# The w2 loads of an expert stage: issued by ScalarE behind the row copy in place of SyncE's queue

## The chip, the core and the metric

The kernel runs on one core of a Trainium2 chip. The metric is the device time of one execution in microseconds, lower is better. A core has TensorE (PE), VectorE (DVE), ScalarE (ACT), GpSimd (POOL) and SyncE (SP), each with an instruction stream of its own; they meet only at semaphores. SyncE, ScalarE and GpSimd can issue DMAs, and each has a queue of its own for them.

## What is computed

The kernel is one layer of a diffusion backbone for 640 tokens of width 1024: modulated normalisation, two attention branches, and then a mixture of 64 small SwiGLU experts with 8 experts per token. The change is in the last part alone:

```python
def swiglu(x, w1, w3, w2):
    return (jax.nn.silu(x @ w1) * (x @ w3)) @ w2

def run_block(args):
    xb, e = args                                   # 128 rows of one expert
    return swiglu(xb, w_e1[e], w_e3[e], w_e2[e])
...
return jax.ops.segment_sum(yd * wd[:, None], td, num_segments=t)
```

w1 and w3 are 1024 x 256, w2 is 256 x 1024, all in float32, so each is 1 MB, and no weight is used by more than one block unless an expert has over 128 rows.

## The kernel before

The stage around the change is the block that begins at L1707. It goes over 64 blocks of 128 rows, one for each expert, and then over overflow blocks for experts with more than 128 rows (in this run 70 blocks in all; the number `nb` is known only on the chip). For block n:

- GpSimd gathers its 128 token rows into `xg` (L1793), and three blocks later scatters the weighted output rows from `yb` into `sums` with an add (L1807). Rows that are empty in the block are left out.
- TensorE transposes the rows (`turn_x`, L1831), multiplies them with w1 and w3 (`up`, L1823 to L1825), transposes the product (`turn_g`, L1849) and multiplies it with w2 (`down`, L1843). In its program step n is: turn_x(n), down(n-2), turn_g(n-1), up(n).
- The multiplication with w1 and w3 is made of three products of rounded halves. ScalarE rounds x (`take_x`, L1879) and the weights (`hi_w13`, L1873), VectorE subtracts to get the rest (L1931, L1924).
- ScalarE also copies the output row block to `yb` (`take_y`, L1892), the transposed product (`take_g`, L1898), and computes silu (L1905). Its step n is: take_x(n), hi_w13(n+1), take_y(n-2), take_g(n-1), silu(n).

The weights go through a ring of four slots (`RING`), each with room for w1, w3 (one semaphore `s_w13[u]`) and w2 (`s_w2[u]`). SyncE issues all of these loads. Its step n waits until the up-projection of block n-4 is done (semaphore `u`) and issues two DMAs for w1 and w3 of block n (L1490); then it waits until the down-projection of block n-5 is done (semaphore `y`) and issues one DMA for w2 of block n-1 (L1494). For the overflow blocks (`late`, L1747) it reads the expert's number from memory (L1749), loads w1 and w3 of block n, and then waits for down(n-4) and loads w2 of block n.

The order in which the engines walk the blocks is in `run` (L1712): eight blocks are written out, blocks 8 to 59 are a hardware loop without conditions, and blocks from 60 on (`LAST` = 15, times four) are a loop in which each part of a step stands under a condition on `nb`.

Of the kernel before, what the change touches and what calls it, by code (L numbers as in the profile page):

```python
# [47 lines left out]
NE, TOPK, NG, TOPG = 64, 8, 8, 4  # L48
# [5 lines left out]
NBLK = NE + OVF  # L54
RING = 4
# [37 lines left out]
def build(nc, I, O, S, ctx):  # L93
    def sb(name, shape, dt=F32):
        return ctx.enter_context(nc.sbuf_tensor(name, shape, dt))

    def sem(name):
        return ctx.enter_context(nc.semaphore(name))
# [1154 lines left out]
    SH = RING - 1  # L1253
# [215 lines left out]
    ove = sb("ove", [1, P], I32)  # L1469
# [18 lines left out]
    def load_w13(sp, n, u):  # L1488
        for a in range(2):
            sp.dma_start(w13[u][:, a], w13_src[a][:, bass.ds(n, 1)].rearrange("p e k n -> p (e k) n"))\  # L1490
              .then_inc(s_w13[u], 16)

    def load_w2(sp, n, u):
        sp.dma_start(w2[u], w2_src[:, bass.ds(n, 1)].rearrange("p e f n -> p (e f) n")).then_inc(s_w2[u], 16)  # L1494
# [17 lines left out]
    se = {n: sem(f"s_e_{n}") for n in names}  # L1512
# [8 lines left out]
    def wslot(tab, n, w):  # L1521

        return tab[:, bass.ds(n, 1), w:w + 1].rearrange("p n w -> p (n w)")
# [183 lines left out]
    with nc.Block() as block:  # L1707


        LAST = NE // RING - 1  # L1710

        def run(eng, step):  # L1712

            for n in range(2 * RING):
                step(n, n // RING, n % RING, lambda k, n=n: None if n >= k else False)
            with eng.Fori(2, LAST) as i:
                for u in range(RING):
                    step(RING * i + u, i, u, lambda k: None)
            nb = eng.value_load(nblk[0:1, 0:1], min_val=NE, max_val=NBLK)
            with eng.Fori(LAST, NBLK // RING + 1) as i:  # L1720
                with eng.If(RING * i - 3 < nb):
                    for u in range(RING):
                        n = RING * i + u
                        step(n, i, u, lambda k, n=n: n - k < nb)
            return nb

        def due(eng, cond, what):
            if cond is None:
                what()
            elif cond is not False:  # L1730
                with eng.If(cond):
                    what()

        @block.sync
        def _(sp):

            def step(n, u):
                if not (isinstance(n, int) and n < SH):
                    if not (isinstance(n, int) and n < RING):
                        sp.wait_ge(se["u"], n - RING + 1)  # L1740
                    load_w13(sp, n, u)
                if not (isinstance(n, int) and n <= SH):
                    if not (isinstance(n, int) and n <= RING):
                        sp.wait_ge(se["y"], n - RING)
                    load_w2(sp, n - 1, (u - 1) % RING)

            def late(n, u):  # L1747

                e = sp.value_load(ove[0:1, bass.ds(n - NE, 1)], min_val=0, max_val=NE - 1)  # L1749
                sp.wait_ge(se["u"], n - RING + 1)  # L1750
                load_w13(sp, e, u)
                sp.wait_ge(se["y"], n - RING + 1)
                load_w2(sp, e, u)

            for n in range(RING + 1):
                step(n, n % RING)
            for u in range(1, RING):
                step(RING + u, u)
            with sp.Fori(2, NE // RING) as i:
                for u in range(RING):  # L1760
                    step(RING * i + u, u)
            sp.wait_ge(se["y"], NE - RING)
            load_w2(sp, NE - 1, RING - 1)
            nb = sp.value_load(nblk[0:1, 0:1], min_val=NE, max_val=NBLK)
            with sp.Fori(NE // RING, NBLK // RING) as i:
                with sp.If(RING * i < nb):
                    for u in range(RING):
                        n = RING * i + u
                        with sp.If(n < nb):
                            late(n, u)  # L1770

        @block.gpsimd
        def _(pool):
# [8 lines left out]
            def step(n, i, u, guard):  # L1782
# [29 lines left out]
                due(pool, guard(3), scatter)  # L1812

            nb = run(pool, step)

            pool.wait_ge(s_sc[0], (nb + 1) // 2 * 16)
# [3 lines left out]
        def _(pe):  # L1820
# [6 lines left out]
            def step(n, i, u, guard):  # L1827
# [35 lines left out]
                due(pe, guard(0), up)  # L1863

            run(pe, step)

        @block.scalar
        def _(act):
            def hi_w13(n, i, u):

                act.wait_ge(s_w13[u], 32 * (i + 1))
                for a in range(2):
                    act.activation(wHi13[u % 2][:, a], w13[u][:, a], ACT.Copy).then_inc(se["h13"], 1)  # L1873

            def step(n, i, u, guard):
                def take_x():
                    act.wait_ge(se["Tx"], n + 1)
                    for h in range(2):
                        act.activation(xHi[:, 4 * h:4 * h + 4, :].rearrange("p k t -> p (k t)"),  # L1879
                                       pX[:, 512 * h:512 * (h + 1)], ACT.Copy).then_inc(se["xh"], 1)  # L1880

                def next_w13():
                    if not (isinstance(n, int) and n == 0):
                        act.wait_ge(se["u"], n)
                    hi_w13(n + 1, i + (u + 1) // RING, (u + 1) % RING)

                def take_y():
                    m = n - 2
                    act.wait_ge(se["y"], m + 1)
                    if not (isinstance(n, int) and m < 2):  # L1890
                        act.wait_ge(s_sc[u % 2], 32 * i + 16 * ((u - 2) // 2))
                    act.activation(yb[u % 2], pY, ACT.Copy, scale=wslot(tabs, m, 2).bitcast(F32)).then_inc(se["ye"], 1)  # L1892

                def take_g():
                    act.wait_ge(se["Th"], n)
                    if not (isinstance(n, int) and n < 2):
                        act.wait_ge(se["y"], n - 1)
                    act.activation(gT.rearrange("p f t -> p (f t)"), pG[:, 0:256], ACT.Copy).then_inc(se["te"], 1)  # L1898

                def silu():  # L1900
                    act.wait_ge(se["u"], n + 1)
                    if not (isinstance(n, int) and n == 0):

                        act.wait_ge(se["g"], n)
                    act.activation(hs, pH[:, 0:FE], ACT.Silu).then_inc(se["sl"], 1)  # L1905

                due(act, guard(0), take_x)
                due(act, guard(-1), next_w13)
                due(act, guard(2), take_y)
                due(act, guard(1), take_g)  # L1910
                due(act, guard(0), silu)


            act.wait_ge(s_acc, 16 * NT)
            hi_w13(0, 0, 0)
            run(act, step)

        @block.vector
# [135 lines left out]
```

## Time and profile before

| | |
|---|---|
| median of the runs before | 1903.27 us (1901.7, 1903.27, 1909.15) |
| the profiled execution, its own time | 1898.28 us |
| its span, first to last instruction | 1896.5 us |
| PE busy | 1688.7 us, 89% of the span |
| ACT busy | 698.6 us, 37% |
| DVE busy | 860.4 us, 45% |
| POOL busy | 528.2 us, 28% |
| bytes moved by DMA | 351.65 MB, mean 185 GB/s |
| the expert stage | about 1078 to 1860 us of the span |

Times below are microseconds from the start of the span. PE, DVE, ACT and POOL are the engines, PEld is TensorE's weight load. SPq, ACTq and so on are what an engine's sequencer does (issuing a DMA, register work), which isn't counted as busy. "idle before <-releaser" behind an instruction is the time that its engine stood idle before it, and what ended that idle time. In the tables of stretches, PEclk is the granted TensorE clock as a share of its full speed, and the DMA share is the mean busy share of the core's 16 DMA engines. The times that a releaser is given are inferred from semaphore events, and an idle engine that isn't the bottleneck costs nothing.

### The profile page before, as it was taken

The page shows a single profiled execution, that of the slowest core. Times are in us where ns is not written, and L with a number is a line of the kernel's source. Part 1 is how long each engine was busy: PE and PEld are TensorE (multiplying, and loading weights), DVE is VectorE, ACT ScalarE, POOL GpSimd, SP SyncE. Part 2 cuts the span into 40 slices and gives each one's busy share as a digit, 9 for nine tenths or more (in the row PEclk, how much of TensorE's full clock was granted, in tenths as well). Part 3 has the DMA queues.
Part 4 walks back from the last instruction along what each step waited for, and adds up shares of the span by engine and source line. Part 5 has one row for each costly group of instructions (what it writes and reads, how often), then busy time and mean ns, then how long its engine had stood idle before and what let it go on. Part 6 is the DMA issues. An engine that isn't in the chain of part 4 may idle for free. (4 is left out here: it accounts for less than half of the span.)

```text
span 1896.5 us, 23413 instructions
## 1 busy us (share of the span) xinstructions
PE 1688.7 (89%) x8047; PEld 1182.5 (62%) x8047; DVE 860.4 (45%) x1296; ACT 698.6 (37%) x1002; POOL 528.2 (28%) x629
## 2 busy tenths in 40 slices
PE   7979999769999799999987499999899899998991
PEld 2457767456666599997453266666666566666660
DVE  2444454454455500210563266655555555555553
ACT  3112223222232411310220266655555555555550
POOL 0010000020010233331007234444444444444440
PEclk9989999989999999999988799999999999999996
DMA  9411212200000323224334399999999999999954
GB/s 333 141 45 45 88 48 85 79 22 1 0 0 0 111 67 88 67 69 152 135 144 157 108 329 366 373 354 333 331 337 337 328 333 334 331 322 332 322 200 168
DMA packets 119810, 351.65 MB, mean 185 GB/s; under 512 B 20858, under 2 KB 60366, under 8 KB 92760
## 3 DMA queue, kind: packets, MB, share of 16 engines
q1 hardware_dynamic: 97610, 306.42, 43.7%
q0 software_dynamic: 21440, 42.08, 9.4%
q10 hardware_dynamic: 720, 2.62, 0.3%
q8 instruction: 24, 0.39, 0.1%
q14 instruction: 16, 0.13, 0.0%
HBM read 334.63 MB, written 47.87 MB: 202 GB/s over the span
## 5 line engine op out<-in xcount | busy, mean ns | idle before, releaser
L1924 DVE TENSOR_TENSOR e_wlo<-mem,e_whi 128x2048 fp32r<-128x2048 f32 x140 | 314.6, 2288 | 315.5 <-ACT e_whi L1873 315.5
L1873 ACT ACTIVATE e_whi<-mem 128x2048 fp32r<-128x2048 f32 x140 | 260.3, 1909 | 275.3 <-DMA mem<-in_w_e 266.3
L1843 PE MATMUL psum<-mem 128*128 128x512 f32 x560 | 255.6, 599 | 50.0 <-ACT mem L1898 49.8
L1780 POOL TENSOR_TENSOR held<-nhalf 1x1 f32<-1x1 f32 x206 | 136.8, 664 | 366.0 <-ACT mem_h L1892 182.1
L1823 PE MATMUL psum<-e_whi,e_xhi 128*128 128x512 f32 x560 | 228.1, 407 | 7.1 <-DVE e_xlo L1931 7.1
L1825 PE MATMUL psum<-e_wlo,e_xhi 128*128 128x512 f32 x560 | 222.0, 396 | 0.0
L1824 PE MATMUL psum<-e_whi,e_xlo 128*128 128x512 f32 x560 | 221.9, 396 | 0.0
L1843 PEld LDWEIGHTS psum<-mem 128*128 128x128 f32 x560 | 100.8, 190 | 160.5 <-issue 144.1
L764 ACT ACTIVATE mem<-psum,small 128x640 f32<-128x640 f32 (+1 forms) x80 | 56.7, 708 | 242.8 <-DVE small L863 242.7
L1823 PEld LDWEIGHTS psum<-e_whi,e_xhi 128*128 128x128 f32 x560 | 105.7, 189 | 30.1 <-DVE e_xlo L1931 7.8
L1825 PEld LDWEIGHTS psum<-e_wlo,e_xhi 128*128 128x128 f32 x560 | 105.5, 188 | 25.5
L1824 PEld LDWEIGHTS psum<-e_whi,e_xlo 128*128 128x128 f32 x560 | 105.9, 189 | 22.4
L863 DVE TENSOR_REDUCE small<-psum 128x1 f32<-128x640 f32 (+1 forms) x80 | 57.4, 718 | 133.8 <-PE psum L655 86.1
L653 PE MATMUL psum<-mem 128*128 (+2 forms) x288 | 100.1, 448 | 9.3 <-ACT mem L764 7.1
L1931 DVE TENSOR_TENSOR e_xlo<-psum,e_xhi 128x512 fp32r<-128x512 f32 x140 | 89.6, 682 | 7.4 <-ACT e_xhi L1879 7.4
L796 POOL TENSOR_TENSOR small<-small,nhalf 128x5 f32<-128x5 f32 (+1 forms) x16 | 25.0, 1560 | 226.4 <-DVE small L830 114.5
L1129 PE MATMUL psum<-h_hi,w_hi 128*128 128x320 f32 x256 | 80.4, 314 | 7.5 <-DVE h_lo L1196 7.5
L653 PEld LDWEIGHTS psum<-mem 128*128 128x128 f32 x288 | 46.3, 192 | 60.6 <-issue 49.2
L1831 PE MATMUL psum<-ident,mem 128*128 128x128 f32 x560 | 73.4, 274 | 10.1 <-PEq L1525 10.1
L1793 POOL DMA_INDIRECT mem<-h,gi x68 | 72.1, 1061 | 34.7 <-issue 34.7
L684 PE MATMUL psum<-mem 128*128 128x128 f32 x640 | 80.5, 275 | 0.0
L1879 ACT ACTIVATE e_xhi<-psum 128x512 fp32r<-128x512 f32 x140 | 76.3, 605 | 11.2 <-PE psum L1831 10.6
(258 smaller groups left out, 2960.9 us busy)
## 6 DMA issues: line engine op xcount, KB each, us to landing
mem<-in_w_e SPq DMA_DIRECT2D x210, 1024.0 KB
mem<-in_w_mod SPq DMA_DIRECT2D x8, 2048.0 KB, 7.8
mem<-in_w_mod SPq DMA_DIRECT2D x8, 1024.0 KB, 12.0
sums<-mem SPq DMA_DIRECT2D x10, 512.0 KB
mem<-sums SPq DMA_DIRECT2D x10, 512.0 KB, 7.9
mem<-in_x_sample SPq DMA_DIRECT2D x8, 512.0 KB, 11.2
mem<-in_w_in SPq DMA_DIRECT2D x1, 4096.0 KB, 14.7
wkvb<-in_w_in SPq DMA_DIRECT2D x8, 512.0 KB, 4.2
```

The source lines that it names most:

```text
L653: mm = pe.matmul(pS[:, o:o + w], q, kT(c, w), start=True, stop=not mla)
L684: mm = pe.matmul(pO[:, (t - 1) * P:t * P], vh[:, kt, :], pT[:, j, (t - 1) * P:t * P], start=(j == 0), stop=(j == 4))
L1129: pe.matmul(out, whi[b][:, q, k, :], hi[:, k, cols_], start=(k == 0), stop=False)
L1780: pool.tensor_tensor(held[:, c:c + 1], nhalf[0:1, 0:1], nhalf[0:1, 0:1], ALU.add)
L1823: pe.matmul(out, xh, wh, start=first, stop=False)
L1824: pe.matmul(out, xl, wh, start=False, stop=False)
L1825: return pe.matmul(out, xh, wl, start=False, stop=last)
L1843: mm = pe.matmul(pY[:, cs], gT[:, f, :], w2[v][:, f, cs], start=(f == 0), stop=(f == 1))
L1873: act.activation(wHi13[u % 2][:, a], w13[u][:, a], ACT.Copy).then_inc(se["h13"], 1)
L1879: act.activation(xHi[:, 4 * h:4 * h + 4, :].rearrange("p k t -> p (k t)"), pX[:, 512 * h:512 * (h + 1)], ACT.Copy).then_inc(se["xh"], 1)
L1924: dve.tensor_tensor(wLo13[u][:, a], w13[u][:, a], wHi13[u % 2][:, a].bitcast(F32), ALU.subtract)\
L1931: dve.tensor_tensor(xLo[:, 4 * h:4 * h + 4, :].rearrange("p k t -> p (k t)"), pX[:, 512 * h:512 * (h + 1)], xHi[:, 4 * h:4 * h + 4, :].bit ...
```

## The change

ScalarE issues the w2 loads. Its step n, behind take_y(n-2), gets a new part `next_w2`, which loads w2 of block n+2 into the slot that down(n-2) has just left free; the row copy has waited for the same semaphore `y` just before, so no wait is added. The parts exist for n >= 2; for n+2 >= 64 the expert's number is read from memory. SyncE keeps the loads of w1 and w3, w2 of block 3, and (outside of what is changed) w2 of blocks 0 to 2. Its waits on `y` and its w2 loads go, in the steps and in `late`. In `run`, blocks 60 to 63 are now written out on every engine, and the loop with conditions begins at block 64.

```diff
@@ run
             nb = eng.value_load(nblk[0:1, 0:1], min_val=NE, max_val=NBLK)
-            with eng.Fori(LAST, NBLK // RING + 1) as i:
+            for n in range(RING * LAST, NE):
+                step(n, LAST, n % RING, lambda k, n=n: None if n - k < NE else n - k < nb)
+            with eng.Fori(LAST + 1, NBLK // RING + 1) as i:
@@ sync
             def step(n, u):
-                if not (isinstance(n, int) and n < SH):
-                    if not (isinstance(n, int) and n < RING):
-                        sp.wait_ge(se["u"], n - RING + 1)
-                    load_w13(sp, n, u)
-                if not (isinstance(n, int) and n <= SH):
-                    if not (isinstance(n, int) and n <= RING):
-                        sp.wait_ge(se["y"], n - RING)
-                    load_w2(sp, n - 1, (u - 1) % RING)
+
+                if not (isinstance(n, int) and n < RING):
+                    sp.wait_ge(se["u"], n - RING + 1)
+                load_w13(sp, n, u)
 
             def late(n, u):
 
                 e = sp.value_load(ove[0:1, bass.ds(n - NE, 1)], min_val=0, max_val=NE - 1)
                 sp.wait_ge(se["u"], n - RING + 1)
                 load_w13(sp, e, u)
-                sp.wait_ge(se["y"], n - RING + 1)
-                load_w2(sp, e, u)
-
-            for n in range(RING + 1):
-                step(n, n % RING)
-            for u in range(1, RING):
-                step(RING + u, u)
-            with sp.Fori(2, NE // RING) as i:
+
+            step(SH, SH)
+            load_w2(sp, SH, SH)
+            with sp.Fori(1, NE // RING) as i:
                 for u in range(RING):
                     step(RING * i + u, u)
-            sp.wait_ge(se["y"], NE - RING)
-            load_w2(sp, NE - 1, RING - 1)
@@ scalar, step
+                def next_w2():
+                    if guard(-2) is None:
+                        load_w2(act, n + 2, (u + 2) % RING)
+                    else:
+                        e = act.value_load(ove[0:1, bass.ds(n + 2 - NE, 1)], min_val=0, max_val=NE - 1)
+                        load_w2(act, e, (u + 2) % RING)
+
...
                 due(act, guard(2), take_y)
+                if not (isinstance(n, int) and n < 2):
+                    due(act, guard(-2), next_w2)
                 due(act, guard(1), take_g)
```

## Rows read from the trace of the kernel before

**Rows 1.** Windows: stretch, length, busy us per engine, PEclk, DMA share, GB/s.
```profile
1110.00:1240.00 130.00, 130.00 (x540) 89.96 (x540) 78.55 (x64) 79.11 (x88) 62.46 (x90) 1.00 1.01 366
1300.00:1700.00 400.00, 363.82 (x1473) 247.61 (x1474) 216.31 (x176) 220.28 (x250) 175.44 (x246) 1.00 0.97 332
```

**Rows 2.** Timeline of ACT, one early block: start, us, engine, line, operation.
```profile
1111.91 0.38 ACT L1905 ACTIVATE mem<-psum 128x256 f32<-128x256 f32 x1 [3.31 <-PE psum L1825]
1117.36 1.11 ACT L1892 ACTIVATE mem<-psum,mem 128x1024 f32<-128x1024 f32 x1
1122.04 0.38 ACT L1905 ACTIVATE mem<-psum 128x256 f32<-128x256 f32 x1 [3.30 <-PE psum L1825]
```

**Rows 3.** Instructions of L1490 from 1250 to 1745 us (duration ns min/median/max).
```profile
L1490 SPq DMA_DIRECT2D mem<-in_w_e x88: 332/347/430, 1254.0 to 1743.9; - x88
```

**Rows 4.** Who waited for whom: total us, times, longest; last row L1873 alone, 1250-1745.
```profile
POOL held L1780 <- ACT mem_h L1892: 175.4, 34, 7.0
POOL held L1780 <- ACT mem L1892: 173.6, 34, 7.7
PE psum L1843 <- ACT mem L1898: 48.3, 42, 3.1
...
  DMA mem<-in_w_e: 226.3, 44
```

**Rows 5.** Timeline of a later block, SyncE, ACT, GpSimd and PE.
```profile
1401.56 0.81 SPq L1490 DMA_DIRECT2D mem<-in_w_e  x2
1402.06 1.09 ACT L1892 ACTIVATE mem<-psum,mem 128x1024 f32<-128x1024 f32 x1
1407.23 0.33 SPq L1494 DMA_DIRECT2D mem<-in_w_e  x1
1407.66 1.06 POOL L1793 DMA_INDIRECT mem<-h,gi  x1 [0.51 <-issue]
1412.76 1.09 ACT L1892 ACTIVATE mem_h<-psum,mem 128x1024 f32<-128x1024 f32 x1
1413.19 0.81 SPq L1490 DMA_DIRECT2D mem<-in_w_e  x2
1423.54 1.03 PE L1831 MATMUL psum<-ident,mem 128*128 128x128 f32 x8
1431.41 3.72 ACT L1873 ACTIVATE e_whi<-mem 128x2048 fp32r<-128x2048 f32 x2 [4.21 <-DMA mem<-in_w_e]
```

**Rows 6.** DMA queues (packets, MB, share of 16 engines): 1110-1240, then 1300-1700.
```profile
q1 hardware_dynamic: 5218, 38.06, 71.8%
q0 software_dynamic: 3470, 9.38, 28.7%
...
q1 hardware_dynamic: 15206, 110.75, 73.8%
q0 software_dynamic: 10067, 21.93, 23.3%
```

**Rows 7.** Timeline at the end of the list: ACT's rounding, SyncE's issues.
```profile
1761.69 0.82 SPq L1490 DMA_DIRECT2D mem<-in_w_e  x2
1770.72 0.82 SPq L1490 DMA_DIRECT2D mem<-in_w_e  x2
...
1771.28 3.73 ACT L1873 ACTIVATE e_whi<-mem 128x2048 fp32r<-128x2048 f32 x2 [4.32 <-DMA mem<-in_w_e]
1784.80 3.71 ACT L1873 ACTIVATE e_whi<-mem 128x2048 fp32r<-128x2048 f32 x2 [7.28 <-DMA mem<-in_w_e]
```

**Rows 8.** Windows as rows 1, at the end of the list.
```profile
1751.00:1762.00 11.00, 11.00 (x47) 7.73 (x46) 6.22 (x5) 6.89 (x9) 5.00 (x7) 1.00 0.75 267
1784.00:1795.00 11.00, 7.90 (x33) 5.02 (x33) 6.13 (x5) 6.86 (x8) 4.59 (x5) 1.00 0.82 300
1795.00:1806.00 11.00, 11.00 (x47) 7.76 (x46) 6.28 (x6) 7.93 (x9) 5.39 (x10) 1.00 0.93 327
```

**Rows 9.** Issue of one DMA, and the read of an expert's number (ns min/median/max).
```profile
L1494 SPq DMA_DIRECT2D mem<-in_w_e x70: 327/333/578, 981.3 to 1824.0; - x70
L1971 ACTq DMA_DIRECT2D out_ys<-mem x4: 338/338/339, 1882.5 to 1893.4; - x4
L1749 SPq TENSOR_LOAD <-ove x6: 40/282/352, 1760.9 to 1814.5; - x6
```

**Rows 10.** The page's queue of ScalarE, whole span.
```profile
q10 hardware_dynamic: 720, 2.62, 0.3%
```

## The prediction, made before the result was known

> **What bounds the kernel now.** I read the trace first by stretch, then by wait, then by block. In the windows the expert stage shows two regimes: from 1110 to 1240 us PE is busy all the time, from 1300 to 1700 us only 364 of 400 us, at the full clock in both [rows 1]. The first regime is one block per 10.14 us: that is the distance of two silu instructions (L1905), and ACT idles 3.3 us in each before it [rows 2]. In the second regime SyncE issues 44 pairs of w1/w3 loads from 1254.0 to 1743.5 us, so a block takes 489.5 / 43 = 11.38 us [rows 3]. What ended the idle time there is a load: in that stretch ACT's rounding of w1/w3 waits 226.3 us in 44 blocks for the DMA [rows 4]. PE itself loses 48 us in the whole stage, and it loses them one hop further on, waiting for the copy of the turned products (L1898), which stands behind the late rounding in ACT's program [rows 4].
>
> Is the load late because it is issued late, or because the DMA engines are full? Two readings say full. The w1/w3 pair of block 33 is issued at 1401.56 and used at 1431.41 [rows 5]: 29.9 us for 2 MB, with two blocks' loads standing ahead of it. And from 1300 to 1700 us SyncE's queue takes 73.8% and GpSimd's 23.3% of the 16 engines' time, together 97.1% [rows 6]. Per block (11.4 us) that is 105 MB-loads in 35 blocks, three each: 400 x 0.738 / 105 = 2.81 us of all engines per 1 MB load, 8.4 us for three, and 400 x 0.233 / 35 = 2.7 us for one gather and one scatter; 11.1 of 11.4 us. In the early stretch the same sums give 130 x 0.718 / 39 = 2.39 us per load and 10.0 us per block, so even there the engines are full; the ring's lead of loaded blocks only hides it until about 1250 us. **The stage is bound by the DMA engines' time**, with PE 11% behind. The rows give a mean over the 16 engines; they do not show whether some lag behind others.
>
> **The change part by part.** The bytes, the packets and the number of loads stay: 70 w2 loads of 1 MB, of which 66 (blocks 4 to 69) move from SyncE's queue to ScalarE's. As the engines' time is the bound, the sum begins at zero and takes up what is moved on the way.
>
> (a) *SyncE loses its waits on the w2 slots.* In the steady loop these waits hold nothing back: w2's issue comes 5.7 us after the pair's, and the next pair waits 6.0 us more for the end of the up-projection [rows 5]. 0 us. SyncE's own issue time (0.33 us) was idle time anyway.
>
> (b) *When the w2 load is issued.* Before: at the moment PE ends the down-projection (1407.23). After: behind the row copy L1892, which stands behind the rounding L1873, so the same slot is refilled at 1412.76 + 1.09 = 1413.85, 6.6 us later [rows 5]. It is needed four blocks after that, some 45 us. 0 us for w2 itself.
>
> (c) *The order among the loads.* This is the term that counts. In one queue w2(n-1) stands behind w13(n) and both wait some 30 us. GpSimd's gather does not: issued at 1407.66 behind the scatter, its rows are used from 1423.54 on without a wait [rows 5], 15.9 us, while SyncE's backlog is twice that. So a second queue is served beside the first, and the new w2 load will overtake the backlog. w2 then runs one to two blocks ahead of where it was, and each w2 that is moved ahead of a w1/w3 pair delays this pair by the engines' time of 1 MB, 2.4 to 2.8 us. That is a shift, paid once, not per block, and at the end of the stage it is partly given back, since the last w2 loads are then already in. What is left is read at the last gate that holds PE. This is the pair of block 64: its rounding begins at 1784.80, 13.5 us after that of block 63 [rows 7], and PE works 7.9 of 11 us there and all of the next 11 us [rows 8]. Before, the w2 loads up to 63 stand ahead of it. After, also that part of w2(64) which moves before it is complete: w2(64) is issued about 5.7 us after the rounding of block 63 begins, so 5 to 6 us before the next pair is in. Bounds: nothing (0) and the whole load (2.8); I take two thirds of 2.6, **+1.7 us**.
>
> (d) *ScalarE's own time.* An issue costs 0.33 us on SyncE's queue and 0.34 to 0.40 us on ScalarE's [rows 9], plus register moves of 0.03 to 0.05. It stands between L1892 and L1898, for which PE waits. In a block paced by PE it is hidden by the 3.3 us of idle time before silu [rows 2]. In a block paced by the DMA it makes PE's down-projection 0.4 us later; the slot of this block is then released 0.4 us later, which only shortens the time that the next request waits in a backlog of two blocks. Cover: this backlog. Without it the cost would be 43 x 0.4 = 17 us. From block 64 on the expert's number must also be read from memory: 0.28 us and some 0.1 of register work [rows 9]. Once, at the gate of block 64, both are on PE's path: 0.34 + 0.28 + 0.1 + 0.1 = **+0.8 us**.
>
> (e) *The end of SyncE's list.* Before, w13(64) is issued at 1761.69, after a wait for w2(63)'s slot, and w13(65) at 1770.72 behind w2(64) [rows 7]. After, both go out when the up-projection ends, some 5 us earlier. If the engines had nothing of this in their queue then, it was worth something: the mean share falls to 0.75 from 1751 to 1762 us [rows 8]. But the pair of block 63 was still to land (rounded at 1771.28), so the engines that end last had work. 0 us, with a bound of -3 us: PE's loss of 3.1 us in that window [rows 8] is all there is to gain.
>
> (f) *Four blocks written out (60 to 63)* on every engine, in place of a loop with conditions. PE is busy 100% in the eight written-out blocks at the start, fetching included [rows 1]. 0 us.
>
> Sum: +1.7 + 0.8 = +2.5 us, so 1898.28 + 2.5 = 1900.8 for an execution like the profiled one (span 1896.5). That execution is 5 us under the median of the runs, 1903.27, against which the result is measured: **1905.8 us**. 0.5% is 9.5 us, about what can be told from no change here.
>
> **The rivals.**
> *A. The gather becomes the gate (slower).* While a w2 load moves, GpSimd's packets would share each engine with two queues and not with one. The Trainium skill (DMA: Bandwidth & Descriptors, Queues, rings and completion order) says that each DMA engine goes round the queues that have work, a packet at a time; no row here shows the order of turns. The loop is: row copy ends (1403.15), gather issued (1407.66, 4.5 us), landing G, turn of x, and by the PE-paced block 6.6 us from the end of the up-projection to the next row copy's end [rows 2, 5]. It spans three blocks, 34.2 us, so it decides only from G = 34.2 - 4.5 - 6.6 = 23 us. Now G is at most 15.9. A w2 load in the way adds 2.6 us to the scatter ahead of it and 2.6 to the gather: 21 us, just short. At G = 26 each block would be 1 us longer: 43 us, 1946; at G = 24, 14 us, 1918. For it: little margin is left. Against it: GpSimd waits for the row copy, not for DMAs, in 349 us [rows 4], and a late gather brings the row copy forward.
>
> *B. The second queue fills the engines' gaps (faster).* 2.9% of the engines' time is free from 1300 to 1700 us [rows 6]. If that were gaps within SyncE's queue that another queue can fill, 0.33 us per block and 43 blocks give -14 us: 1889. Against it: the queue holds 30 us of work, and the bytes stay.
>
> *C. Only the end of the list counts.* (e) at its bound: 1903.3 + 0.8 - 3 = 1901.
>
> *D. The order costs more.* Two whole w2 loads ahead of block 64's pair at a third of a block each (3.8 us) and 0.4 us in some blocks of the last stretch: +9, 1912.
>
> **How the numbers follow.** Forecast 0.65, C 0.13, D 0.07, A 0.08, B 0.07. The forecast with its bounds (0 to 2.8, 0.4 to 1.5) is 1903.5 to 1908, and the runs before spread by 3 us around such values; C and D take it to 1900 and 1912. With half of A's mild end the range is 1898 to 1914. Faster by over 0.5% is B: 0.07. Slower is A and a part of D: 0.10. Same: 0.83.
>
> **What would show it.** Right: ScalarE's queue (now only the five stores at the end, 2.62 MB [rows 10]) carries some 69 MB, SyncE's some 69 MB less, and the 16 engines' total share from 1300 to 1700 us stays at 97%; a block stays at 11.4 us; ACT's rounding still waits for the DMA, the first time one or two blocks earlier; w2's issue stands 1.1 us after the row copy's start; the gap before block 64's rounding shrinks from 13.5 to some 11.5 us, since the order is evened out. Wrong: PE waiting at the turn of x (L1831) for the gather (A), a block under 11.2 us with a share of 99% (B), or a row copy that ends later than 0.5 us before L1898, an issue that blocks ScalarE. By the page of the skill named above, section Issuing engines are not separate DMA queues, a second issuing engine saves only issue time; by that the sum is (d) alone, +0.8, and the rows of SyncE's idle time agree that there was no issue time to save.

## The result: 0.64% faster, outside the stated range

| | before | after |
|---|---|---|
| median of 8 runs each | 1903.70 us (1898.49 to 1909.15) | 1892.65 us (1888.00 to 1897.42) |
| ratio, 95% interval | 1 | 0.9936 [0.9922, 0.9951] |
| the profiled execution, its span | 1896.5 us | 1892.0 us |
| stage, rounding of block 12 to that of block 60 | 545.4 us | 528.8 us |
| block, mean of blocks 20 to 60 | 11.42 us | 11.00 us |

Forecast was 1905.8 us, in a range of 1898 to 1914; the time is 5.4 us below its lower end and 13 us below the forecast. Against the median before it is 11 us, which is more than the 9.5 us that I called measurable.

The block times in this text are all read in one way: the starts of ScalarE's rounding of w1/w3, one pair of instructions per block. First the windows of after, the stretches of [rows 1] (columns as there).

```profile
1110.00:1240.00 130.00, 128.26 (x529) 87.86 (x528) 80.94 (x65) 81.59 (x89) 64.33 (x85) 1.00 1.00 360
1300.00:1700.00 400.00, 376.42 (x1530) 252.92 (x1530) 232.30 (x184) 238.12 (x257) 171.33 (x256) 1.00 0.97 344
```

From 1300 to 1700 us PE works 376.4 us where it worked 363.8, and the DMA engines move 344 GB/s where they moved 332. The share is 0.97 in both. So the same busy share moved 3.6% more bytes. The queues of after in that stretch (packets, MB, share of 16 engines) answer to [rows 6]; behind them stand ScalarE's issue line L1494 from 1250 us on, and two rows from the list of DMA issues on the page of after (KB each, median us from issue to landing; w1 and w3 share a semaphore, so the first row's 9.7 us is not the landing of a whole pair).

```profile
q1 hardware_dynamic: 10476, 76.32, 49.0%
q10 hardware_dynamic: 5286, 38.52, 26.4%
q0 software_dynamic: 10431, 22.61, 21.9%
...
L1494 ACTq DMA_DIRECT2D mem<-in_w_e x45: 339/339/340, 1252.4 to 1737.0; - x45
...
mem<-in_w_e SPq DMA_DIRECT2D x144, 1024.0 KB, 9.7
mem<-in_w_e ACTq DMA_DIRECT2D x66, 1024.0 KB, 11.1
```

The change does what it says: 66 of the 210 loads are on ScalarE's queue, at 0.34 us an issue.

Where did the wait go? The rounding line of after, 1250 to 1745 us (ns min/median/max, first and last start), and under it what it waited for; it answers to the last row of [rows 4]. Then the waits of after from 1300 to 1700 us (total us, times, longest).

```profile
L1865 ACT ACTIVATE e_whi<-mem x91: 1897/1912/1917, 1248.7 to 1744.3; 128x2048 fp32r<-128x2048 f32 x91
  DMA mem<-in_w_e: 3.9, 12
...
POOL held L1772 <- DMA sums<-mem_h,si: 74.1, 18, 4.9
POOL held L1772 <- DMA sums<-mem,si: 71.8, 18, 4.6
ACT mem_h L1884 <- DMA sums<-mem_h,si: 27.6, 18, 2.2
ACT mem L1884 <- DMA sums<-mem,si: 27.1, 18, 2.0
PE psum L1823 <- DMA mem<-h,gi: 23.5, 31, 1.3
```

The weights are hardly waited for any more: 3.9 us in 12 blocks, where it was 226.3 us in 44. In their place stand GpSimd's own transfers: GpSimd (L1772) and the row copy (L1884) wait for the scatter of two blocks before, 146 and 55 us of 400, and PE at the turn of x (L1823) waits for the gather, 23.5 us in 31 blocks. The gate has moved from the weights to the rows. In one block of after it looks like this (timeline, columns as [rows 5]):

```profile
1412.37 1.06 POOL L1785 DMA_INDIRECT mem<-h,gi  x1 [0.51 <-issue]
1412.37 3.72 ACT L1865 ACTIVATE e_whi<-mem 128x2048 fp32r<-128x2048 f32 x2
1417.38 1.12 ACT L1884 ACTIVATE mem_h<-psum,mem 128x1024 f32<-128x1024 f32 x1 [1.29 <-DMA sums<-mem_h,si]
1417.53 0.34 ACTq L1494 DMA_DIRECT2D mem<-in_w_e  x1
1418.39 0.38 ACT L1897 ACTIVATE mem<-psum 128x256 f32<-128x256 f32 x1
1420.95 1.09 PE L1823 MATMUL psum<-ident,mem 128*128 128x128 f32 x8 [0.48 <-DMA mem<-h,gi]
```

The rounding starts without a wait. The row copy waits 1.3 us for the scatter, the load of w2 goes out 0.15 us after the copy's start, and the copy of the turned products (L1897) follows the row copy with no gap: the issue, 0.34 us on ScalarE's sequencer, costs its compute nothing here, nor in any of the 27 blocks from 1300 to 1600 us. The gather takes at most 8.6 us, 1412.37 to 1420.95.

### The profile page after: what moved, and what is told of

It reads as the page before. It is cut to its first block and busy times, and to the rows that moved or that the text cites. A ratio compares the mean times of both kernels' runs of the same rounds, so it can differ in the third digit from the quotient of the medians.

```text
span 1892.0 us, 23323 instructions
## 1 busy us (share of the span) xinstructions
PE 1695.4 (90%) x8047; PEld 1182.7 (63%) x8047; DVE 874.3 (46%) x1296; ACT 712.7 (38%) x1003; POOL 520.8 (28%) x629
## 5 line engine op out<-in xcount | busy, mean ns | idle before, releaser
L1772 POOL TENSOR_TENSOR held<-nhalf 1x1 f32<-1x1 f32 x206 | 115.5, 561 | 288.9 <-DMA sums<-mem_h,si 120.1
L1942 DVE TENSOR_TENSOR mem<-mem,psum 128x256 f32<-128x256 f32 x70 | 42.5, 608 | 159.2 <-ACT mem L1904 153.2
L1823 PE MATMUL psum<-ident,mem 128*128 128x128 f32 x560 | 76.2, 280 | 44.2 <-DMA mem<-h,gi 33.7
L1823 PEld LDWEIGHTS psum<-ident,mem 128*128 128x128 f32 x560 | 62.1, 142 | 69.0 <-DMA mem<-h,gi 54.7
## 6 DMA issues: line engine op xcount, KB each, us to landing
mem<-in_w_e ACTq DMA_DIRECT2D x66, 1024.0 KB, 11.1
mem<-in_x_sample SPq DMA_DIRECT2D x8, 512.0 KB, 11.2
```

Source lines behind the costliest of these rows:

```text
L1772: pool.tensor_tensor(held[:, c:c + 1], nhalf[0:1, 0:1], nhalf[0:1, 0:1], ALU.add)
L1823: tr = pe.transpose(pX[:, k * P:(k + 1) * P], xg[u % 2][:, k * P:(k + 1) * P], ident[:, :])
```

## The experiments

All ratios are to the kernel before, run on the same chip in turn; chips differ (medians of before 1904.7, 1890.1, 1891.8 and 1903.5 us in the four sets), so times of different sets aren't compared. In the edits, `y` is the end of the down-projection, `ye` the end of the row copy, `u` the end of the up-projection and `sl` silu. The line with the ratio is followed by the block time of blocks 20 to 60 from one profile; before gave 11.42 and 11.36 us in two profiles and after 11.00 and 10.99, so differences of some 0.06 us say nothing.

What an edit did to the requests is read from its trace: the median time, from 1300 to 1600 us, from the end of the up-projection that frees the slot to the issue of w1/w3, and from the end of the down-projection to the issue of w2. It is 0.2 and 0.0 us in before, and 0.2 and 3.2 us in after.

### First set: which part of the change?

**Blocks 60 to 63 written out, and nothing else.**

```diff
+            for n in range(RING * LAST, NE):
+                step(n, LAST, n % RING, lambda k, n=n: None if n - k < NE else n - k < nb)
-            with eng.Fori(LAST, NBLK // RING + 1) as i:
+            with eng.Fori(LAST + 1, NBLK // RING + 1) as i:
```

> The kernel before with one part of the change alone: blocks 60 to 63 written out in the order of the blocks. All loads stay in SyncE's queue. If the gain is in the loads (my theory: the two queues), the time is that of before, 1903 us within 3, and a block takes 11.4 us. If it is in the written-out blocks, the time falls to 1893.

Measured: 1905.13 us, 1.0004 [0.9992, 1.0016]; block 11.37 us. Edit (f) is worth nothing, and all of the gain belongs to the loads.

**SyncE keeps the w2 loads, but asks for them only when the row copy is done.** (Meant to be as late as in the changed kernel.)

```diff
-                        sp.wait_ge(se["y"], n - RING)
+                        sp.wait_ge(se["ye"], n - RING)
```

(and likewise in `late` and for block 63.)

> The kernel before, but SyncE issues each w2 load only when the row copy of the slot's last block is done (semaphore ye in place of y), so at the time at which ScalarE issues it after the change, in one queue still. Theory 'second queue': 1903 us, 11.4 us per block. Theory 'later request' (w2 asked for some 6 us later, away from the others): 1893 us, 11.0 us per block.

Measured: 1901.62 us, 0.9991 [0.9977, 1.0004]; block 11.23 us. The rounding from block 60 to 69 takes 95.8 us in place of 93.3, since in `late` SyncE's next pair now stands behind the later wait. The trace shows that the edit moved more than it was meant to: w2 is asked for 7.3 us after the down-projection (3.2 in after), and the w1/w3 pair, which stands behind it in SyncE's program, 2.2 us after the up-projection in place of 0.2. One block of this kernel, the row copy and what SyncE issues behind it:

```profile
1406.71 1.09 ACT L1892 ACTIVATE mem<-psum,mem 128x1024 f32<-128x1024 f32 x1
1407.98 0.33 SPq L1494 DMA_DIRECT2D mem<-in_w_e  x1
1408.58 0.81 SPq L1490 DMA_DIRECT2D mem<-in_w_e  x2
```

So later requests of all loads, in one queue, shorten the block by some 0.15 us, not by 0.4, and the end of the list gives part of it back; the time of the kernel is that of before.

**The roles swapped: ScalarE issues w1 and w3 behind silu, SyncE issues w2.** (Against the changed kernel.)

```diff
-                sp.wait_ge(se["u"], n - RING + 1)
-                load_w13(sp, n, u)
+                sp.wait_ge(se["y"], n - RING + 1)
+                load_w2(sp, n, u)
+                def ring_w13():
+                    load_w13(act, n + 4, u)
...
                 due(act, guard(0), silu)
+                due(act, guard(-4), ring_w13)
```

> The queues exchanged: ScalarE issues w1 and w3 behind silu, SyncE issues w2 as soon as the down-projection is done (about as early as before the change). Theory 'second queue', whichever engine has which load: 1893 us, 11.0 us per block. Theory 'later request': 1903 us, since w2 is asked for early again. ScalarE's 0.7 to 0.8 us for two issues are hidden in both.

Measured: 1895.82 us, 0.9959 [0.9946, 0.9972]; block 11.09 us. Here w2 is asked for early, on `y`, and w1/w3 too, although their issue stands behind silu in the program: ScalarE's sequencer issues it 0.15 us after silu's start.

```profile
1411.46 0.38 ACT L1903 ACTIVATE mem<-psum 128x256 f32<-128x256 f32 x1 [1.88 <-PE psum L1816]
1411.61 0.86 ACTq L1490 DMA_DIRECT2D mem<-in_w_e  x2
```

The requests come 0.2 and 0.2 us after the two ends, as in before. So this is a second queue with the moments unchanged, and the block is 0.3 us shorter.

**All loads on ScalarE's queue: w1 and w3 behind silu, w2 as in the change. One queue.** (Against the changed kernel; `ring_w13` as above, and `next_w2` stays.)

```diff
-                if not (isinstance(n, int) and n < RING):
-                    sp.wait_ge(se["u"], n - RING + 1)
-                load_w13(sp, n, u)
...
                 due(act, guard(0), silu)
+                due(act, guard(-4), ring_w13)
```

> One queue again, but ScalarE's: w1 and w3 behind silu, w2 behind the row copy as after the change. Theory 'second queue': 1903 us or a little more (three issues of ScalarE per block), 11.4 us per block. Theory that the issuing engine or the time of the issue counts: 1893 us, 11.0 us per block.

Measured: 1895.33 us, 0.9957 [0.9944, 0.9970]; block 11.13 us. One queue again, and two thirds of the gain are there, with w1/w3 asked for 0.2 us and w2 2.7 us after the two ends. So most of the gain can be had with a second queue and without one. The line of the rounding, 1300 to 1600 us, of the kernel with all loads on ScalarE's queue, and then of the one with the roles swapped:

```profile
L1843 ACT ACTIVATE e_whi<-mem x54: 1895/1910/1920, 1304.5 to 1595.3; 128x2048 fp32r<-128x2048 f32 x54
  DMA mem<-in_w_e: 131.9, 27
...
L1864 ACT ACTIVATE e_whi<-mem x54: 1898/1910/1915, 1305.9 to 1594.3; 128x2048 fp32r<-128x2048 f32 x54
  DMA mem<-in_w_e: 17.4, 26
```

With one queue the weights still come last (131.9 us of waits in 27 blocks), with two they don't (17.4); yet the blocks are nearly equal, 11.13 and 11.09 us. Which transfer ends last does not set the pace here.

### Second set: are all 16 engines full?

The landing of the loads made me doubt this. Each 1 MB load leaves 16 events on its semaphore in the trace. In before, from 1300 to 1550 us, half of the events of a w1/w3 pair had come 7.9 us (median) after its issue, and the last after 30.8 us; for w2 it was 7.6 and 29.9 us. One half of the engines is done with a load while the other half is 22 us behind. The packets in flight say the same: from 1300 to 1600 us their number falls under 8 in 0.01% of the time, but it is 8 to 11 in 5.8% and 15 or more in 86%. That fits eight engines that hardly ever pause beside eight that do.

The Trainium skill (DMA: Bandwidth & Descriptors, The descriptor swizzle) has in a 1 MiB transfer to 128 partitions each engine write groups of four neighbouring partitions, engine 0 to 7 partitions 0 to 63 and engine 8 to 15 the rest, each group of four and the one 32 further on to one engine. Together with this kernel's order of rows, that names the eight: the table of row numbers is loaded so that row s of a block sits in partition 8(s mod 16) + s div 16. From [rows 6], 21.93 MB / 35 blocks / 2 transfers / 4096 bytes = 76.5 rows per block are in use, and the first 64 of them sit in the partitions with p mod 8 < 4, every other group of four. By this rule of the Trainium skill eight engines carry 64 of 76 rows of each gather and scatter, and the other eight 12. The trace doesn't hold the engine of a packet, so the rule was put to a run.

**Before, with the rows laid over the partitions in another order**, so that the used rows fall evenly on the groups of four. Bytes, packets and waits stay.

```diff
-            sp.dma_start(tabs[:, 0:NBLK, :], S["slots"].rearrange("(r a n) w -> a r n w", a=16, n=NBLK))\
-              .then_inc(s_tab, 16)
+            tsrc = S["slots"].rearrange("(g j h e n) w -> h g e j n w", g=2, j=4, h=2, e=8, n=NBLK)
+            for h in range(2):
+                for g in range(2):
+                    sp.dma_start(tabs[64 * h + 32 * g:64 * h + 32 * g + 32, 0:NBLK, :], tsrc[h, g]).then_inc(s_tab, 16)
-            pool.wait_ge(s_tab, 16)
+            pool.wait_ge(s_tab, 64)
```

> The kernel before with another order of rows in a block: the table of slots is loaded so that row s of a block stands in partition 64*(s//8 % 2) + 32*(s//64) + 4*(s % 8) + (s//16 % 4), in place of 8*(s % 16) + s//16. An expert has 80 rows on average, so before, partitions with p % 8 below 4 are full and the others nearly empty. Theory 'half of the DMA engines': eight of the 16 engines carry nearly all of GpSimd's rows and set the pace; with the rows spread evenly a block falls from 11.4 us to the 10.14 us of PE, 47 blocks x 1.25 = 59 us, so about 1846 us. Theory 'all engines are full' (my prediction's): the bytes and packets are the same, so 1903 us.

Measured: 1831.46 us against 1890.1, 0.9698 [0.9678, 0.9717]; block 10.14 us. That is the PE-paced block of [rows 2], now through the whole stage. The last event of a w1/w3 pair comes 11.0 us after its issue in place of 30.8, and half of them after 8.1; 8 to 11 packets are in flight in 0.2% of the time and 15 or more in 99%. The windows and queues of this kernel, 1300 to 1600 us:

```profile
1300.00:1600.00 300.00, 300.00 (x1249) 208.79 (x1248) 188.88 (x148) 186.21 (x208) 146.65 (x206) 1.00 1.02 375
...
q1 hardware_dynamic: 12899, 93.92, 75.0%
q0 software_dynamic: 8577, 18.67, 26.8%
```

PE is busy 300 of 300 us and the engines move 375 GB/s. So the 97% of [rows 6] were not 97% of what the engines can move. One packet of the loads (8 KB) took 314 ns here (300 x 16 x 0.75 / (93.92 MB / 8192)), but by the same sum 349 ns in [rows 6]: 400 x 16 x 0.738 / (110.75 MB / 8192). Before's busy share was high because its packets were slower, not because there were more of them.

**The changed kernel with the same order of rows.**

> The changed kernel with the same order of rows. Theory 'half of the engines': PE sets the pace here too, so 1846 us, the same as with the queues of before, and the change is worth nothing any more. Theory 'the second queue makes DMAs faster in itself': 11 us below the kernel before with the same rows, or, if PE is the bound, the same. Theory 'all engines are full': 1892 us.

Measured: 1836.26 us, 0.9710 [0.9694, 0.9727]; block 10.14 us. Where PE sets the pace, the change is worth nothing in the block, and the kernel is 4.8 us slower with it.

**Before, and then after, with 6 of the 24 matmuls of each up-projection** (k = 0 and 7 of eight; the other 18 are left out, so PE no longer bounds anything).

```diff
-                    for k in range(KT):
+                    for k in (0, KT - 1):
```

> The kernel before with 6 of the 24 matmuls of each up-projection (k = 0 and k = 7 alone, so three quarters of that product is left out); PE then needs some 5 us per block. The loads, gathers and scatters are all there. If DMA engines set the pace in blocks 13 to 60, a block still takes 11.4 us, and the blocks before take it too: the stage is no more than 10 us shorter. If PE's work stands in the chain that sets the pace, a block gets shorter.

> The changed kernel with the same 6 of 24 matmuls. Theory 'the service of the slow engines got better': 11.0 us per block again, 0.4 us under the kernel before with the same cut. Theory that only the coupling with PE changed: no difference to the kernel before with the cut.

Measured: 1863.11 and 1870.0 us, one run each; blocks of 11.02 and 11.07 us. Their windows, before's order of loads first:

```profile
1300.00:1600.00 300.00, 214.83 (x660) 118.21 (x660) 165.29 (x136) 168.27 (x189) 135.59 (x193) 0.81 0.97 346
...
1300.00:1600.00 300.00, 214.68 (x651) 124.55 (x650) 172.65 (x136) 172.78 (x190) 139.12 (x189) 0.81 0.96 343
```

PE is busy 215 of 300 us, and neither mean block is under 11.0 us (single blocks spread from 9.6 to 12.5). So 11.0 us is what the DMA engines need for a block, with the rows on the crowded half. The changed kernel runs at that floor (11.00). The kernel before stood 0.4 us above it, but only with PE at full work: with less of it, before comes down to the same floor by itself. That is the term I had at nothing.

### Third set: does the gain hold, and do two queues serve better?

**After and before again, as they are, on another chip.**

> The changed kernel as it is, once more beside the kernel before. The runs before this one came from two chips, on which the kernel before took 1904.7 and 1890.1 us. If the gain is the same share on any chip: 0.6% again. If it depends on how far the eight loaded DMA engines lag on that chip, it is smaller where the kernel before is quicker: 0.6% at 1904, 0 to 0.3% at 1890.

> The kernel before, for a trace on this chip. Its block time goes with its time: 11.4 us at 1904, 11.1 us at 1890.

Measured: after 1880.89 us, 0.9944 [0.9926, 0.9962], block 10.99 us; before 1893.45 us, 1.0010 [0.9995, 1.0024], block 11.36 us. The chip is 12 us quicker than that of the first result, and the block times are within 0.06 us of those there. The expectation for before, a block of 11.1 us, was wrong: chips differ outside of this stage. The same pair gives the sum without the noise between chips, from one profile each:

| us | before | after | difference |
|---|---|---|---|
| start to the second rounding | 1077.1 | 1076.5 | -0.6 |
| from there to block 12 | 113.5 | 112.3 | -1.2 |
| block 12 to 60 | 543.7 | 528.8 | -14.9 |
| block 60 to 69 | 92.5 | 93.1 | +0.6 |
| to the end of the span | 64.1 | 66.9 | +2.8 |
| span | 1890.9 | 1877.6 | -13.3 |

**Both with the even order of rows and 6 of 24 matmuls** (18 left out), so that neither the crowded half nor PE sets the pace.

> Even rows and 6 of the 24 matmuls of each up-projection, loads all in SyncE's queue: PE needs some 5 us per block, so the DMA engines' own pace shows with the work spread over all 16. From the packets (24 of 0.31 us and 4.8 each of 0.16 and 0.33 us per engine) 9.8 us per block, against 11.0 with uneven rows.

> The same with the changed queues. Theory 'a second queue serves better by itself': clearly under the run beside it, 9.4 against 9.8 us per block. Theory 'it only helps where eight engines lag': the same within 0.1 us.

Measured: 1793.59 us, 0.9482 [0.9455, 0.9508], block 9.86 us; and 1799.33 us, 0.9512 [0.9486, 0.9538], block 9.95 us. Windows in the same order:

```profile
1300.00:1600.00 300.00, 224.21 (x730) 124.56 (x729) 187.46 (x154) 190.26 (x216) 150.93 (x212) 0.86 1.02 389
...
1300.00:1600.00 300.00, 225.95 (x724) 130.01 (x723) 191.09 (x152) 193.25 (x212) 174.44 (x211) 0.85 1.02 381
```

With all 16 engines evenly loaded, a second queue moves 381 GB/s and one queue 389. Two queues do not serve better by themselves. The gain of the change needs a crowded half and a busy PE.

### Fourth set: the steps between before and the floor

**SyncE asks for w1/w3 behind silu in place of the up-projection; then that and w2 on `ye`.** One queue, all on SyncE.

```diff
-                        sp.wait_ge(se["u"], n - RING + 1)
+                        sp.wait_ge(se["sl"], n - RING + 1)
```

> The kernel before, with one semaphore changed: SyncE asks for w1 and w3 when silu is done, some 2 us later, and for w2 as before. One queue, SyncE's. If the time of the w1/w3 request counts: a block goes from 11.4 to about 11.2 us. If it does not: 11.4 us, 1.000 of before.

> Both requests late in SyncE's queue: w1 and w3 behind silu, w2 behind the row copy, which are the times at which ScalarE alone issued them in e4. If only the times count, this is e4: 11.13 us per block, 0.996 of before. If ScalarE's queue is served better than SyncE's, it is e2: 11.23 us, 0.999.

Measured: 1900.14 us, 0.9981 [0.9964, 0.9998], block 11.21 us; and 1902.97 us, 0.9993 [0.9981, 1.0006], block 11.18 us, with 95.9 us from block 60 to 69 (93.5 in the first of the two). The requests come 2.1 and 0.0 us after the two ends in the first, 2.2 and 7.2 us in the second. So the gain comes with w1/w3 asked for 2 us later; asking for w2 7 us later as well adds nothing that can be told.

**All loads on ScalarE's queue, again.**

> e4 once more, so that it stands on one chip with the run before this one: 0.996 of before and 11.13 us per block on any chip.

Measured: 1895.82 us, 0.9958 [0.9942, 0.9975]; block 11.14 us, as in the first set. The kernel just above was meant to ask for its loads at the same points, by another engine, but it doesn't: 0.2 and 2.8 us after the two ends here, 2.2 and 7.2 there. So the pair doesn't separate the issuing engine from the moment. Of its lead of 7 us, 3.9 are at the end of the list (92.0 against 95.9 us from block 60 to 69, where SyncE's next pair stands behind its wait for the row copy), and 3.6 lie between blocks 12 and 60 (533.8 against 537.4), which single profiles can hardly tell apart.

**Before with 12 of 24 matmuls** (k = 0, 1, 2 and 7; the other 12 are left out).

> The kernel before with 12 of the 24 matmuls of each up-projection (k = 0, 1, 2 and 7; half of the product left out). Between 24 (11.37 us per block) and 6 (11.02): if the surplus of 0.35 us goes with PE's time it is 11.1 to 11.2 us here; if it needs PE to be nearly full, 11.0.

Measured: 1878.69 us, one run; block 11.05 us. The 0.4 us above the floor are gone when PE does half of its up-projection:

```profile
1300.00:1600.00 300.00, 232.45 (x813) 139.98 (x814) 166.99 (x136) 170.13 (x194) 135.90 (x190) 0.90 0.97 344
```

In sum (requests: us after the end of the up-projection for w1/w3, of the down-projection for w2):

| loads | w1/w3 asked | w2 asked | us per block |
|---|---|---|---|
| before: one queue, SyncE's | 0.2 | 0.0 | 11.36 to 11.42 |
| one queue, SyncE's | 2.1 | 0.0 | 11.21 |
| one queue, SyncE's (two kernels) | 2.2 | 7.2, 7.3 | 11.18, 11.23 |
| one queue, ScalarE's (two runs) | 0.2 | 2.7, 2.8 | 11.13, 11.14 |
| two queues, roles swapped | 0.2 | 0.2 | 11.09 |
| two queues, the change | 0.2 | 3.2 | 10.99, 11.00 |
| floor: before and after with less work on PE | | | 11.02 to 11.07 |

**What stays open.** By which route the block of before comes to stand above the floor. Three things take the excess away, wholly or in part: less work on PE; later requests in one queue; a second queue with the requests where they were. No run asks for w2 alone some 3 us later in SyncE's queue, so how much of ScalarE's one queue is the moment and how much the engine that issues isn't shown either.

The packets don't settle it. From 1300 to 1600 us, in the trace's own list of packets, the median 8 KB packet takes 309 ns in every kernel here; what differs is a tail. Over 400 ns take 8.4% of them in before, 5.2% in after, 3.7% in before with 6 of 24 matmuls, 1.1% with even rows. In before the tail stands behind the requests: 24% of the packets that start 1 to 2 us after a w1/w3 request are that long, 3% of those 3 to 5 us after it. These are the moments at which the eight engines that were ahead start again, so the slow packets may well be theirs and not those of the crowded ones; no view shows it. And the mean packet is no measure of the pace: it is 347 ns in before and 341 in after (the sum over 1300 to 1700 us gives 349, and 337 and 359 for SyncE's and ScalarE's loads in after), but 335 in SyncE's two kernels that wait for silu, whose blocks are longer than those of after.

## Why the prediction was wrong, by its steps

- **What bounds the stage: half right.** The DMA engines do set it: the block stays at 11.0 us when three quarters of the up-projection are left out. But "the engines are full" was wrong. Eight of them were; the others were 22 us ahead and paused at times, and slow packets filled the share. I wrote that the rows "do not show whether some lag behind others" and went on as if none did. The rows held two warnings. One: the same load costs 2.39 us of all engines in the early stretch and 2.81 us later; I used both numbers and didn't ask why equal packets should cost 18% more. Two: 366 GB/s at a share of 1.01 against 332 at 0.97 [rows 1], so 4% less share moved 9% less.
- **The term that was mis-sized** is the per-block one. I set it at zero because bytes and packets stay. Measured, it is -0.37 us per block on one chip and -0.42 in the other pair of profiles, -14.9 and -16.6 us from block 12 to 60, and it is the whole result. The zero would have held if all 16 engines had been full at a constant time per packet; neither was so (eight paused at times, and the mean 8 KB packet took 349 ns with crowded rows and 314 with even ones).
- **(a) SyncE's waits go: right.** They held nothing back. **(b) w2 asked for later: the 6.6 us were wrong, and the price of 0 isn't shown.** It was asked for 3.2 us after the down-projection's end, 0.15 us after the row copy's start and not 1.1: the sequencer doesn't wait for the copy. Between the roles swapped and the change, which asks 3 us later for w2, lie 0.1 us per block, but the queues differ too; SyncE's 7 us later were worth nothing beside w1/w3's 2 us.
- **(c) The order of the loads: mechanism right, effect wrong.** w2 does overtake: it lands in 11.2 us in place of 29.9. But w1/w3 isn't pushed back by that, it lands 24.1 us after its issue in place of 30.8. The +1.7 us at the gate of block 64 didn't come: its rounding begins 10.7 us after that of block 63, where it was 13.5.
- **(d) ScalarE's issue: right on the block; the +0.8 can't be told from 0.** Issues take 0.34 us beside a running copy. From block 60 to 69 it is 93.3 before and 93.1 us after, 92.5 and 93.1 on the other chip.
- **(e) and (f), the end of the list and the written-out blocks: right, 0 us** (1.0004 for the latter; no run has (e) alone, but blocks 60 to 69 take as long as before).
- **After the stage** after is 4.4 and 2.8 us longer in the two pairs. I had nothing there. One profile of before with blocks 60 to 63 written out shows the same (67.1 us against 62.9), and its time is no longer for it; I didn't follow it further.
- **Rival A** (gather as the gate, slower): its sign was in the trace and its cost was not. PE waits for the gather in 31 blocks, for 23.5 us, but G is at most 8.6 us, far from the 23 us from which I let it decide. It waits because GpSimd, held by its scatters, asks late.
- **Rival B** had the size, 1889 us, and the wrong mechanism. Nothing was filled: the share stays 97%, and 8 to 11 packets are in flight in 5.9% of the time (1300 to 1600 us) where it was 5.8%, as the share was to stay if B was wrong. I gave it 0.07 since "the bytes stay"; they did, at 344 in place of 332 GB/s. What the trace would have allowed is to take the early stretch's 2.39 us per load as a bound of this term, 3 x 0.42 = -1.3 us per block, cut off at PE's 10.14 us. The range would then have reached far below 1889.
- **The rule of the Trainium skill** that I set beside the end (DMA: Bandwidth & Descriptors, Issuing engines are not separate DMA queues: more issuing engines save only issue time) gave +0.8 us. The runs bear it out where the engines are evenly loaded (9.86 and 9.95 us) and where PE sets the pace (10.14 and 10.14). On the crowded engines with PE at full work it didn't hold: two queues gave -0.6% as in the change and -0.4% with the roles swapped and the requests at unchanged moments, and moving all loads to ScalarE's one queue gave -0.4% too, though SyncE had issue time to spare in before.

## What to carry to other kernels

A DMA busy share near 1 is not a rate: hold it against GB/s, and work out the time of one packet in two stretches; where equal packets differ, the share may hold waiting that an edit can take away, and "bytes stay, so time stays" is no argument. After an edit of a wait, read from the trace when each request goes out: here an engine that works in order moved the loads behind the edited one too, and an issue that stood behind a computation in the program went out while it ran. Look at how the partitions of row gathers and scatters fall on the 16 engines before touching queues: here another order of rows was worth 3.0% and made the 0.6% of this change vanish. Laying the rows out evenly on the kernel before is the version that beats both, 0.9698 [0.9678, 0.9717].

## What the runs showed of the hardware

- Eight engines can run more than 20 us ahead of the other eight on the same loads: half of a w1/w3 pair landed after 7.9 us, all of it after 30.8 us.
- Equal 8 KB packets took 314 ns in the mean with even rows and 349 ns with crowded ones, at the granted clock of 1.00 in both; the engines together moved 375 GB/s (above) and 334. The latter is from the windows of before on the chip of the third set:

```profile
1300.00:1600.00 300.00, 273.97 (x1115) 187.10 (x1113) 159.18 (x130) 164.13 (x184) 130.61 (x185) 1.00 0.97 334
```

- The moment of a request whose last bytes land some 30 us later still counts: w1/w3 asked for 2 us later in SyncE's queue made the block 11.21 us in place of 11.36 to 11.42.
- ScalarE's sequencer issued a load 0.15 us after the start of the silu or the row copy that stands before it in its program. Behind the row copy, the next computation followed without idle time in all 27 blocks from 1300 to 1600 us.
